# Two tiles of silu(z) of the pooling branch made as a pair of half products, and the last rotation table made earlier

## The reference

```
proj = h @ w_in
u_pool, z_pool, u_ssm, z_ssm, g_pool, g_ssm = split(proj)
y_pool = causal_pool_mixer(u_pool, pool_w, pool_scale) * silu(z_pool)
y_ssm  = s5_mixer(u_ssm, ...) * silu(z_ssm)      # complex diagonal scan, gelu, sigmoid GLU
merged = sigmoid(g_pool) * (y_pool @ w_branch_pool) + sigmoid(g_ssm) * (y_ssm @ w_branch_ssm)
out    = x + gate * rmsnorm(merged @ w_out, norm_post)
```

## Time and profile before

| | us |
|---|---|
| time, median of 3 runs | 956.12 (955.86 to 956.6) |
| the profiled execution, its own time | 956.51 |
| its span, first to last instruction | 954.7 |
| PE busy | 933.3 |
| DVE busy | 633.6 |
| ACT busy | 349.0 |
| mean granted TensorE clock | 0.999 |

### The profile page before, as it was taken

The page is one execution under the profiler, slowest core; times in us unless marked ns, Lnnn a source line. Parts: engine busy times, 40 slices in busy tenths (PEclk is TensorE's granted clock), DMA queues, the critical chain, the costliest instruction groups (busy, mean ns, idle before and its releaser), DMA issues.

```text
span 954.7 us, 11591 instructions
## 1 busy us (share of the span) xinstructions
PE 933.3 (98%) x4420; PEld 784.8 (82%) x4420; DVE 633.6 (66%) x904; ACT 349.0 (37%) x448; POOL 45.3 (5%) x82
## 2 busy tenths in 40 slices
PE   3999999999999999999999999999999999999997
PEld 3888888888888888888888888888888888888885
DVE  5988899877888884577677887665344444455233
ACT  5851353334444443345353535341022231223111
POOL 0019800000000000000000000000000000000000
PEclk9999999999999999999999999999999999999999
DMA  9843355446555354479474761696543258322222
GB/s 348 300 147 121 126 203 168 155 159 195 173 192 202 141 184 157 114 217 260 132 216 137 208 171 44 192 346 239 185 163 111 89 224 214 135 89 89 89 89 88
DMA packets 95143, 162.51 MB, mean 170 GB/s; under 512 B 38512, under 2 KB 55024, under 8 KB 95088
## 3 DMA queue, kind: packets, MB, share of 16 engines
q1 hardware_dynamic: 85728, 157.31, 50.4%
q10 hardware_dynamic: 9360, 4.46, 1.8%
HBM read 115.59 MB, written 46.14 MB: 169 GB/s over the span
## 4 chain that ended last, share of the span: by engine, by line
PE 97%; DVE 1%; DMA 1%; ACT 0%; SPq 0%; issue 0%; DVEq 0%
PE ps L1932 51%; PE ps L2052 18%; PE ps L2160 9%; PE psb L2052 8%; PE ps L2116 2%; PE psb L2105 1%; PE psb L2103 1%; PE psa L2091 1%; PE psa L2010 1%; PE psa L1932 1%; PE psb L1960 1%; DMA x_tok<-in_x 1%; PE ps L1960 0%; PE psb L2010 0%; PE psa L1960 0%; DVE par_w_p L534 0%
## 5 line engine op out<-in xcount | busy, mean ns | idle before, releaser
L1932 PE MATMUL ps<-bop,w_hi 128*128 128x512 f32 x1184 | 317.7, 390 | 0.2 <-DVE bop L1440 0.2
L1932 PEld LDWEIGHTS ps<-bop,w_hi 128*128 128x128 f32 x1184 | 221.3, 188 | 45.6 <-issue 0.3
L1932 PE MATMUL ps<-bop,w_lo 128*128 128x512 f32 x592 | 182.3, 389 | 0.0
L1932 PEld LDWEIGHTS ps<-bop,w_lo 128*128 128x128 f32 x592 | 111.1, 188 | 23.2
L1392 DVE TENSOR_TENSOR w_lo<-raw,w_hi 128x1024 fp32r<-128x1024 f32 x45 | 55.6, 1236 | 48.5 <-ACT w_hi L1010 48.4
L2052 PE MATMUL ps<-bop,r_hi 128*128 128x512 f32 x256 | 78.8, 389 | 0.0
L1010 ACT ACTIVATE w_hi<-raw 128x1024 fp32r<-128x1024 f32 x45 | 47.4, 1054 | 75.7 <-PE ps L1932 61.9
L2052 PEld LDWEIGHTS ps<-bop,r_hi 128*128 128x128 f32 x256 | 48.0, 188 | 10.0
L2052 PE MATMUL ps<-bop,r_lo 128*128 128x512 f32 x128 | 49.8, 389 | 0.0
L2160 PE MATMUL ps<-wo_hi,y_hi 128*128 128x512 f32 x128 | 49.8, 389 | 0.0
L2160 PE MATMUL ps<-wo_lo,y_hi 128*128 128x512 f32 x128 | 49.8, 389 | 0.0
(11 more groups left out here) (325 smaller groups left out, 1582.3 us busy)
## 6 DMA issues: line engine op xcount, KB each, us to landing
raw<-in_wstream SPq DMA_DIRECT2D x54, 512.0 KB, 4.5
pair_raw<-in_wstream SPq DMA_DIRECT2D x24, 512.0 KB, 4.2
ada<-in_w_ada SPq DMA_DIRECT2D x16, 512.0 KB, 11.5
x_tok<-in_x SPq DMA_DIRECT2D x8, 512.0 KB, 6.3
gs_d<-gt SPq DMA_DIRECT2D x8, 512.0 KB, 4.3
win_d<-win_new SPq DMA_DIRECT2D x8, 512.0 KB, 2.7
wout_d<-wout_new SPq DMA_DIRECT2D x8, 512.0 KB, 3.8
wout<-wout_d SPq DMA_DIRECT2D x8, 512.0 KB, 6.0
```

What stands on the lines that cost most here:

```text
L1932: last = mm(ps[slot(u)][:, f * HALF:f * HALF + HALF], a[:, k, :], b(k, f), start=k == order[0] and q == 0, stop=k == order[-1] and q == 2)
```

## The change

The tiles `zp` 4 and `zp` 5 become a pair, which stands in front of the pairs `zp` 0 and `zp` 2, so there are fourteen. Their silu goes to a new DRAM scratch `zp_d` as other pairs' results do, and is loaded back in step 2. `FILL` loses them, and `zp` 6 moves from step 6 to step 4. Since there is one more pair, the places for VectorE's chunks are two more, and the fourth pair of tables, which was made at the start of step 0 in buffers of its own, takes them. So that the last pair still ends in the same buffers, everything that alternates with the pair's number is turned round: the banks of PSUM, the two buffers of raw weights, and the ring, which now starts at slot 1. For the first pair this puts P5 in slot 4. In the head the order on VectorE and ScalarE changes with it.

```diff
-PAIRS += [("zp", 0), ("zp", 2)]
+PAIRS += [("zp", 4), ("zp", 0), ("zp", 2)]
-FILL = {0: [("zs", 7)], 2: [("zp", 4)], 4: [("zp", 5)], 6: [("zp", 6)], 7: [("zp", 7)]}
+FILL = {0: [("zs", 7)], 4: [("zp", 6)], 7: [("zp", 7)]}
...
+def ring_slot(j, i):
+    return (7 * j + i + 1) % RING
...
-            return pair_raw[j % 2] if j else pair_first
+            return pair_raw[(j + 1) % 2] if j else pair_first
...
+            even = 1 - j % 2
             if i in (P5, P3):
-                return (ps[0] if j % 2 else ps[1])[:, HALF * (j % 2):HALF * (j % 2) + HALF]
-            if i == P2 and j:
-                return ps[1][:, HALF:D]
-            return ps[0][:, 0:HALF] if j % 2 or i == P2 else psb[:, HALF:D]
+                return (ps[0] if even else ps[1])[:, HALF * even:HALF * even + HALF]
+            if i == P2:
+                return ps[1][:, HALF:D] if j else psb[:, 0:HALF]
+            return ps[0][:, 0:HALF] if even else psb[:, HALF:D]
...
                 elif j == 1:
+                    sp.wait_ge(coef_stored, 16)
+                elif j == 2:
                     for s in range(2):
                         sp.wait_ge(raw_free[s], (len(FIRST) + 1 - s) // 2)
-                elif j == 2:
-                    sp.wait_ge(coef_stored, 16)
...
-                if j and PAIRS[j - 1][0] != "zp":
+                if 0 < j < NP - 1:
                     store_pair(j - 1)
...
-            load_cfp(LAST_TABLE)
...
-                if m == 0:
-                    made(("cos", LAST_TABLE))
-                    made(("sin", LAST_TABLE))
+                if m == 2:
+                    sp.wait_ge(pair_stored[(NP - 3) % 2], 32 * ((NP - 1) // 2))
+                    for n in (4, 5):
+                        sp.dma_start(zp_t[n], zp_d[n]).then_inc(zp_in, 16)
...
             t_high(3)
+            act.wait_ge(gs_stored[0], 16 * 4)
+            evac(("zs", 0), gt[0][:, :], ACT.Silu)
             pair_high(0, P6)
             pair_high(0, P5)
-            act.wait_ge(gs_stored[0], 16 * 4)
-            evac(("zs", 0), gt[0][:, :], ACT.Silu)
...
             dve.wait_ge(coef_stored, 16)
+            t_low(2)
+            t_low(3)
             sum1(0)
             sum2(0)
-            t_low(2)
             sum4(0)
-            t_low(3)
...
-                if m == 0:
-                    cosines(LAST_TABLE)
-                    sines(LAST_TABLE)
                 pooling(m)
```

More of the change, by code:

```diff
@@ L108 @@
     CHUNKS += [("in", b), ("out", b)]
-CHUNKS += [("cos", 1), ("sin", 1), ("cos", 2), ("sin", 2)]
-LAST_TABLE = 3
+for e in (1, 2, 3):
+    CHUNKS += [("cos", e), ("sin", e)]
 CHUNK_AT, n = {}, 0
@@ L301, in build @@
         vta = ssm("vta", [P, GB, CH, SG])
-        cfp_a = ssm("cfp_a", [P, GB, CF - IO])
-        zp_t = [t[:, :] for t in (gt[0], rt[0], gt[1], rt[1])]
+        zp_t = [t[:, :] for t in (gt[1], rt[1], gt[0], rt[0])]
         zp_t += [t[:, :, :].rearrange("p g c -> p (g c)") for t in (cos_pa, sin_pa)]
@@ L372, in build @@
         gate_d = scratch("gate_d", [D])
-        pair_d = {"us": u_d, "gp": gp_d, "zs": zs_d}
+        zp_d = scratch("zp_d", [KT, P, SEQ])
+        pair_d = {"us": u_d, "gp": gp_d, "zs": zs_d, "zp": zp_d}
         def two(name):
@@ L429, in build @@
         reload_in = two("reload_in")
-        gp_in, zs_in = sem("gp_in"), two("zs_in")
+        gp_in, zs_in, zp_in = sem("gp_in"), two("zs_in"), sem("zp_in")
         gated, yz_done = sem("gated"), sem("yz_done")
@@ L770, in load_cfp @@
                     half_p = slice(NS * q, NS * q + NS)
-                    sp.dma_start((cfp if e < LAST_TABLE else cfp_a)[half_p, :, :], coef_d[2 * e + q][half_p, :].rearrange("p (g f) -> p g f", f=CF)[:, :, IO:CF]).then_inc(cfp_in, 16)
+                    sp.dma_start(cfp[half_p, :, :], coef_d[2 * e + q][half_p, :].rearrange("p (g f) -> p g f", f=CF)[:, :, IO:CF]).then_inc(cfp_in, 16)
             def made(chunk):
@@ L777, in made @@
                     sp.wait_ge(cos_ready, b + 1)
-                    sp.dma_start(cos_d[b], (cos_p if b < LAST_TABLE else cos_pa)[:, :, :].rearrange("p g c -> p (g c)")).then_inc(cos_stored, 16)
+                    sp.dma_start(cos_d[b], cos_p[:, :, :].rearrange("p g c -> p (g c)")).then_inc(cos_stored, 16)
                 elif kind == "sin":
                     sp.wait_ge(sin_ready, b + 1)
-                    sp.dma_start(sin_d[b], (sin_p if b < LAST_TABLE else sin_pa)[:, :, :].rearrange("p g c -> p (g c)")).then_inc(sin_stored, 16)
-                    if b + 1 < LAST_TABLE:
+                    sp.dma_start(sin_d[b], sin_p[:, :, :].rearrange("p g c -> p (g c)")).then_inc(sin_stored, 16)
+                    if b + 1 < KT // 2:
                         load_cfp(b + 1)
@@ L1114, in pair_high @@
                     act.wait_ge(pair_sum, 4 * j + s + 1)
-                if o >= RING:
-                    act.wait_ge(st_done, S_POS[divmod(o - RING, 7)] + 1)
+                if n >= RING:
+                    act.wait_ge(st_done, S_POS[divmod(n - RING, 7)] + 1)
                 elif o >= 4:
@@ L1509, in table_parts @@
             def table_parts(e):
-                c, cos, sin, t = (cfp, cos_p, sin_p, vt) if e < LAST_TABLE else (cfp_a, cos_pa, sin_pa, vta)
+                c, cos, sin, t = cfp, cos_p, sin_p, vt
                 return (c[:, :, 0:8], c[:, :, 8:16], c[:, :, 16:32], c[:, :, 32:48],
@@ L1586, in pair_slot @@
             def pair_slot(j, i):
-                o = 7 * j + i
-                if o >= RING:
-                    dve.wait_ge(st_done, S_POS[divmod(o - RING, 7)] + 1)
+                n, o = 7 * j + i, ring_slot(j, i)
+                if n >= RING:
+                    dve.wait_ge(st_done, S_POS[divmod(n - RING, 7)] + 1)
                 elif o >= 4:
@@ L1759, in yp_out @@
                     dve.wait_ge(c21_done, NP - 1 + n // 2)
+                elif n < 6:
+                    dve.wait_ge(zp_in, 32)
                 else:
@@ L2013, in half_product @@
             def half_product(j, i):
-                o = 7 * j + i
+                o = ring_slot(j, i)
                 pe.wait_ge(pair_lo, W_POS[j, i] + 1)
                 if i == P1:
-                    if j == 1:
-                        pe.wait_ge(c11_done, 1)
-                    elif j:
+                    if j == 0:
+                        pe.wait_ge(job_out[0], SLOT[:len(FIRST)].count(0))
+                    elif j >= 2:
                         pe.wait_ge(c21_done, j - 1)
                 elif i == P2:
-                    if j == 0:
-                        pe.wait_ge(job_out[0], SLOT[:len(FIRST)].count(0))
-                    else:
+                    if j == 1:
+                        pe.wait_ge(job_out[1], SLOT[:len(FIRST)].count(1))
+                    if j:
                         pe.wait_ge(c11_done, j)
```

29 lines of the change are left out of this document (12 added, 17 removed).

## The result

The changed kernel takes 958.69 us (median of 10 runs, 957.01 to 959.55) against 956.43 (10 runs, 955.86 to 956.68) of the kernel before in the same comparison: a ratio of 1.0023, 95% interval 1.0013 to 1.0032. A second comparison gave 958.36 against 956.32, 1.0022 [1.0012, 1.0031]. So it is slower, by 2.0 to 2.3 us. That lies inside the range of the forecast (953.6 to 959.1), outside the likeliest case's own (955.0 to 957.8), and just past the bound up to which the forecast calls it the same (958.0): it falls to "slower", to which I gave 0.21. Its profiled execution took 957.88, with a span of 956.1.

The account below looks back on a forecast made before the run. The prediction took TensorE to bound the kernel, busy 933.3 of 954.7 us. Its terms, -2.72 + 2.4 + 0.2 + 0.4 = +0.3 us, gave a forecast median of 956.4 us, range 953.6 to 959.1.

Parts of the forecast that it names:

- likeliest case: A wait at `part_c(2)` takes the gain back: median 956.4 us, own range 955.0 to 957.8, chance 0.64.
- slower: Outcome of a measured time above 958.0 us, chance 0.21.
- Term 1: Stage 4: pairing `zp` 4 and 5 saves one half product, 2.72 us, with no wait in the new pair.
- Term 2: Step 2: without `zp` 4 as cover, TensorE waits 2.4 us at `part_c(2)` for `sq`; bounds 2.2 and 3.0.
- The gain stays: Rival at `part_c(2)`: it waits less or not at all, as VectorE reaches `sq` earlier; 953.8 us, chance 0.15.
- Term 3: First pair: P6 waits 0.2 us for ScalarE's copy of P1; bounds 0 and 1.5, upper if `gs` 7's store is late.
- Term 4: Start of `bp` 0: its fifth step waits 0.4 us for the fifth `in_low`; bounds 0 and 1.
- The gap makes the array slow: Rival: half-rate matmuls behind the wait, at `part_c(2)` and head of `up` 4; 2.6 us more, 959.0, chance 0.09.
- The loads of `zp` 4 and 5, costed at nothing: Step 2: both loads are issued behind the taps and wanted four steps later, so they cost 0.
- The transfers are late: Rival: taps of `part_c(2)` or the store `copy_p1` waits for land 2 to 3 us late; 958.5 us, chance 0.12.

Follow-up runs that it names:

- e7: Changed kernel with `yp_out(1)` and pooling weights' low part later in step 2, `yp_out(6)` and first P1 copy earlier, `zp` 4 and 5 loads in step 4: 953.96 us.
- e2: Changed kernel with `yp_out(1)` moved behind the scans of step 2 and the low part of the pooling's weights behind `sq`: 956.95 us (954.93 to 962.80).
- e8: Changed kernel with the product `zp` 6 in step 2 in place of step 4: 960.33 us.
- e4: Changed kernel with `yp_out(1)` and pooling weights' low part later in step 2, `yp_out(6)` one `in_low` earlier, first P1 copy ahead of P3 and P4: 956.30 us.
- e9: Changed kernel with nine products that nobody reads put in front of the wait of `part_c(2)` for `sq`: 957.34 us.
- e10: Changed kernel with only the two loads of `zp` 4 and 5 moved from step 2 to step 4: 958.86 us.
- e11: Changed kernel unaltered, one more profiled execution: 958.46 us.
- e3: Changed kernel with `yp_out(6)` behind the first `in_low` instead of the second: 957.28 us.
- e6: Changed kernel with `yp_out(1)` and pooling weights' low part later in step 2, and the `zp` 4 and 5 loads in step 4: 954.97 us.

## Why the prediction was right and wrong

- **Term 1, matmuls: right.** 4408 in place of 4420, no wait in the new pair, and -2.2 in `e7`, where the other terms are nearly gone.
- **Term 2, `part_c(2)`: right in mechanism and length.** 2.3 us against 2.4, released by `sq`, hidden taps, `pw_lo` directly followed by the rotation. `e2` and `e8` removed and moved it as the argument asks. "The gain stays" is out. (Its lower bound should have read 2.3 and not 2.2: 470.36 - 468.02.)
- **Term 3, first pair: right.** 0.27 in the first profile against 0.2, and gone in `e4` and `e7`. It is 0.6 in `e9`, `e10` and `e11`, inside the bounds. The store of `gs` 7, on which I had put the upper bound, isn't the reason. In all three ScalarE stands idle for 0.4 us ahead of its copies, for VectorE's second sum, and copies P1 out with no pause behind them; here in `e10`:

```profile
133.49 1.68 ACT L1130 ACTIVATE r_hi<-r_f 128x512 fp32r<-128x512 f32 x3 [0.39 <-DVE r_f L1606]
135.07 0.62 ACT L1130 ACTIVATE r_hi<-pair_first 128x512 fp32r<-128x512 f32 x1
135.60 0.58 ACT L1139 ACTIVATE gt<-ps 128x512 f32<-128x512 f32 x1
```

- **Term 4, `bp` 0: the step was wrong.** It asked only when `in_low` is ready. `bp` 0 also waits for its bank of PSUM, which `yp_out(6)` empties behind two `in_low`. The prediction's own numbers would have given it: first `in_low` at 583.2, 2.28 until `yp_out(6)` (596.49 - 594.21 above) and 1.28 for it make 586.8, where TensorE wants 596.61 - 0.23 - 10.88 = 585.5. The wait is 1.3 and not 0.4, outside my bound of 1, and `e3` gives 1.1 back (0.8 by its profile). The fifth `in_low` with its 0.4 is real and stands behind it.
- **The gap makes the array slow, to which I gave 0.09: it does, in about two of three executions.** With term 4 this is what made the likeliest case wrong. I weighed the rival by the two gaps that the trace had, 15 us and 0.2, priced it at 2.6 from the matmuls at the start, and treated it as happening always or never. It costs 1.63 when it happens, 1.1 in the median. The Trainium skill ("TensorE: Matmul & The Clock Gate", section "What's actually happening") describes an array that gets half its clock pulses after idling; the trace agrees on the factor of two. It puts the half rate at an idle array; in the four profiles here the clock fell 0.3 to 1.5 us behind the first matmul after the wait, when the array was at work again.
- **The loads of `zp` 4 and 5, costed at nothing: right for this kernel** (`e10`), wrong as a judgement of room, since they are the next limit (`e2`, `e6`). "The transfers are late" is out as a cause of the measured time.

With the measured sizes the sum is -2.72 + 2.3 + 0.3 + 1.3 + 1.1 = +2.3, against 2.0 to 2.3 measured. Of the 2 us by which I was low, one is the clock and one the bank. The range held the measured time only because it had been drawn to take in the rivals; the sum itself was short by two causes.

Open are the long executions of `e2` and `e4`, up to 962.80. They went when the loads were moved, but none was profiled. Their mean clocks say that it fell in most of them: of the eight above 958 us seven have 0.994 to 0.997, and one (960.38) has 0.998. That isn't all: the 0.996 of the longest lies some 0.003 below the quick ones, which is 3 us, and it took 7 more than they. Whether `part_b(4)` waited longer in them, and whether the clock fell behind that wait, is not shown.

## What to carry over

When cover is taken from an engine that bounds the kernel, list for its next instructions every condition they wait for, the free bank of PSUM among them, and not only the operands. Count a wait of TensorE of about 2 us for more than its length, since the granted clock may fall behind it. The sign is the mean granted clock of each run (here 0.996 and 0.997 against 0.998 and more); the spread over a few runs is a weak one. Filling the wait with matmuls that nobody reads is a cheap test. And when a wait is removed, look at once at the loads that are issued by what now ends earlier.

## What was unexpected of the hardware

A fall of the granted clock to 0.50 is a matter of chance at one and the same wait. Behind 2.1 us it came in four of six profiles, began 0.3 to 1.5 us behind the first matmul, and cost the same 1.6 us each time (`part_c(2)` took 5.22 us in all four). Behind 3.5 us the one profile has it, from before the first matmul on, and the mean clocks of all five executions (0.996 and 0.997) fit it. Behind the shorter waits no profile has it: the 1.3 us at `bp` 0 stands in ten profiles, the 1.8 and 1.4 us at `part_b(4)` in one each (`e2`, `e4`), all with a granted clock of 1.00 there. The array at the start of the kernel is different: its 24 matmuls at half rate have a granted clock of 1.00 in the windows from 14 to 22 us, so the row of the granted clock does not show that cause.
